# Expert V loads through an fp32 staging tile and a Pool cast, and the expert output added to the residual straight from PSUM

## The reference

```python
q = (h @ w_query).reshape(B, S, PEER_HEADS, 2, PEER_KEY_DIM)
...                                  # 16 of 16384 experts for each of 8 heads, idx and weight g
u = expert_u[it]
act = jax.nn.gelu(jnp.einsum('td,tkd->tk', xt, u))
return jnp.einsum('tk,tkd->td', gt * act, expert_v[it])
```

## Time and profile before

| | |
|---|---|
| time, median of 3 runs | 5994.31 us (5993.89 to 6028.91) |
| profiled execution, its own time | 5995.51 us |
| span of its slowest core (core 5) | 5994.0 us |
| spans of the eight cores | 5978.2 to 5994.0 us |
| first and last matmul of the expert stage | 4107.3 and 5947.7 us |
| PE, DVE, ACT, POOL busy over the span | 57%, 60%, 35%, 3% |

### The profile page before, as it was taken

The page is one execution under the profiler, slowest core; times in us unless marked ns, Lnnn a source line. Parts: engine busy times, 40 slices in busy tenths (PEclk is TensorE's granted clock), DMA queues, the critical chain, the costliest instruction groups (busy, mean ns, idle before and its releaser), DMA issues.

```text
span 5994.0 us, 76025 instructions; the slowest of 8 cores (5978.2 to 5994.0 us)
## 1 busy us (share of the span) xinstructions
PE 3400.3 (57%) x21200; PEld 2093.6 (35%) x21200; DVE 3620.7 (60%) x7629; ACT 2119.5 (35%) x4835; POOL 208.8 (3%) x399
## 2 busy tenths in 40 slices
PE   3333442566644631111121545446999999999996
PEld 1111111344422321111111222224666666666664
DVE  5777653555532338888878999995444444444445
ACT  3555431344421310100011767662333333333333
POOL 0000001000000000000000000001010010000000
PEclk7666665666656765555555555557999999999998
DMA  3112003000021010000000111124343343344332
GB/s 75 42 43 91 0 0 69 18 11 15 8 46 18 1 32 1 0 1 0 0 1 1 85 85 85 85 99 96 71 87 70 64 85 75 64 81 79 68 64 82
DMA packets 101513, 284.26 MB, mean 47 GB/s; under 512 B 9328, under 2 KB 11632, under 8 KB 98928
## 3 DMA queue, kind: packets, MB, share of 16 engines
q0 software_dynamic: 48144, 87.58, 9.7%
q1 hardware_dynamic: 52960, 191.82, 9.2%
HBM read 291.42 MB, written 75.50 MB: 61 GB/s over the span
## 4 chain that ended last, share of the span: by engine, by line
PE 45%; DVE 26%; issue 14%; ACT 10%; DMA 5%; DVEq 0%; ACTq 0%; POOL 0%; POOLq 0%; SPq 0%
PE ps_pO L1101 15%; PE ps_pA L253 15%; PE ps_pj L253 6%; ACT sb_rig L1018 3%; DVE sb_ohj L1010 3%; PE ps_pjb L253 3%; DVE sb_eqi L1013 2%; DVE sb_n_junk L211 2%; DVE sb_eq L973 1%; DVE sb_eq L969 1%; ACT sb_PT L643 1%; PE ps_pW L1029 1%; PE ps_pO L647 1%; DVE sb_sc L934 1%; PE ps_pPT L640 1%
## 5 line engine op out<-in xcount | busy, mean ns | idle before, releaser
L1101 PE MATMUL ps_pO<-sb_vt,sb_gw 128*128 128x512 bf16 x4096 | 1091.8, 379 | 19.0
L1090 DVE TENSOR_TENSOR sb_gw<-sb_ge,sb_wsl 128x256 bf16<-128x256 f32 x1024 | 434.6, 424 | 1057.9 <-PE ps_pO L1101 999.8
L253 PE MATMUL ps_pA<-sb_hfT,sb_ut 128*128 128x256 bf16 x8192 | 1063.5, 273 | 2.2 <-DVE sb_hfT L228 2.2
L253 PEld LDWEIGHTS ps_pA<-sb_hfT,sb_ut 128*128 128x128 bf16 x8192 | 801.7, 98 | 299.7 <-issue 2.4
L1088 ACT ACTIVATE sb_ge<-ps_pA 128x256 f32<-128x256 f32 x1024 | 399.5, 390 | 1207.2 <-PE ps_pA L253 1010.4
L1029 PE MATMUL ps_pW<-sb_rig,sb_ohj 128*128 128x128 bf16 x2048 | 380.9, 288 | 392.7 <-DVE sb_rig L1022 218.2
L1101 PEld LDWEIGHTS ps_pO<-sb_vt,sb_gw 128*128 128x128 bf16 x4096 | 400.1, 98 | 349.4 <-issue 100.4
L1029 PEld LDWEIGHTS ps_pW<-sb_rig,sb_ohj 128*128 128x128 bf16 x2048 | 205.4, 123 | 568.3 <-issue 567.4
L986 PE MATMUL ps_pTs<-sb_ident_f,sb_isel 128*128 128x128 f32 x16 | 7.1, 447 | 693.1 <-DVE sb_isel L976 693.1
L1115 DVE TENSOR_TENSOR sb_x_res<-sb_stage,sb_x_res 128x512 f32<-128x512 f32 x512 | 342.7, 690 | 29.1 <-ACT sb_stage L1109 3.3
L1034 ACT ACTIVATE sb_Wst<-ps_pW 128x512 bf16<-128x512 f32 x512 | 282.0, 593 | 219.7 <-PE ps_pW L1029 210.1
(11 more groups left out here) (208 smaller groups left out, 5090.9 us busy)
## 6 DMA issues: line engine op xcount, KB each, us to landing
wd_scratch<-sb_Wst SPq DMA_DIRECT2D x16, 4096.0 KB, 11.6
sb_wsl<-wd_scratch SPq DMA_DIRECT2D x128, 512.0 KB, 4.4
sb_ut<-uT POOLq DMA_DIRECT2D x128, 256.0 KB, 4.7
sb_vt<-ev POOLq DMA_DIRECT2D x128, 256.0 KB, 4.6
sb_xtmp<-xprev SPq DMA_DIRECT2D x48, 512.0 KB, 3.8
sb_x_res<-xown SPq DMA_DIRECT2D x16, 512.0 KB, 16.4
sb_xtmpb<-xown SPq DMA_DIRECT2D x16, 512.0 KB, 3.5
y<-sb_ot SPq DMA_DIRECT2D x16, 512.0 KB, 2.7
```

The source lines that it names most:

```text
L253: k.op("pe", lambda e, l=l, rh=rh, i=i: e.matmul(out_ap, lhsT=l, rhs=rh, start=(i == 0), stop=(i == n - 1)), r=r, w=w)
L1090: k.op("dve", lambda e: e.tensor_tensor(out=gw_[:].rearrange("p (a t) -> p a t", a=2), in0=ge_[:].rearrange("p (a t) -> p a t", a=2), in1= ...
L1101: k.op("pe", lambda e, po=po, t=t, half=half: e.matmul(po[:], lhsT=gw_[:, t * 128:(t + 1) * 128], rhs=v_[:, i, half * 512:(half + 1) * 512 ...
```

## The change

Three things change, all in the expert stage. `vt` gets one resource per slice (`nres=GS`), and line 1101's matmul of slice i waits only for that slice. V is loaded by `load_v`: SP issues a DMA of one slice in fp32 into one of three staging tiles `vstg`, used in turn, and POOL copies it to `vt`, which makes it bf16. The staging tile is free again when POOL's copy is done. At the end of a block ACT's copies and the tile `stage` are gone: DVE adds each `pO` tile to `x_res`.

```diff
--- before.py
+++ after.py
@@ -1049,12 +1049,21 @@
                 NG = 128 // GS
                 hfT = sb(pc, "hfT", [128, 8, NT], BF16)
                 ut = [sb(pc, "ut%d" % i, [128, GS, 8, 128], BF16) for i in range(2)]
-                vt = [sb(pc, "vt%d" % i, [128, GS, D], BF16) for i in range(2)]
+                vt = [sb(pc, "vt%d" % i, [128, GS, D], BF16, nres=GS) for i in range(2)]
+                vstg = [sb(pc, "vstg%d" % i, [128, D], F32) for i in range(3)]
+                vsc = [0]
+
+                def load_v(v_, i_, gi):
+                    st_ = vstg[vsc[0] % 3]
+                    vsc[0] += 1
+                    k.dma("sp", st_[:], ev_v[:, gi, :], r=[], w=[st_.res], sres=st_.res)
+                    k.op("pool", lambda e: e.tensor_copy(out=v_[:, i_, :], in_=st_[:]), r=[st_.res], w=[v_.rs[i_]])
+
                 uT_v = uT_d.rearrange("(i p) (c e) -> p i c e", p=128, c=8)
                 ev_v = ev_d.rearrange("(i e) d -> e i d", e=128)
                 for i_ in range(GS):
                     k.dma("pool", ut[0][:, i_, :, :], uT_v[:, i_, :, :], r=[], w=[ut[0].res], sres=ut[0].res)
-                    k.dma("pool", vt[0][:, i_, :], ev_v[:, i_, :], r=[], w=[vt[0].res], sres=vt[0].res, max_dma_last_dim=4096)
+                    load_v(vt[0], i_, i_)
                 with ExitStack() as pcn:
                     pTn = [ps(pcn, "pT4%d" % i, [128, 8, 128], BF16) for i in range(2)]
                     norm_pairs([(x_res[:, tile, :], x_res.rs[tile], pTn[tile % 2], hfT[:, :, tile * 128:(tile + 1) * 128], hfT.res)
@@ -1065,7 +1074,6 @@
                 wsl = [sb(pc, "wsl%d" % i, [128, 2, GS, 128], BF16) for i in range(2)]
                 ge = [sb(pc, "ge%d" % i, [128, T3], F32) for i in range(3)]
                 gw = [sb(pc, "gw%d" % i, [128, T3], BF16) for i in range(3)]
-                stage = [sb(pc, "stage%d" % i, [128, 2, D], F32, nres=4) for i in range(2)]
                 wd_v = wd_d.rearrange("t j (i x) -> j t i x", i=128)
                 items = [(g, tb, i) for g in range(NG) for tb in range(NT // T3) for i in range(GS)]
                 state = {}
@@ -1076,7 +1084,7 @@
                     if tb == 0 and i == 0 and g > 0:
                         for i_ in range(GS):
                             k.dma("pool", u_[:, i_, :, :], uT_v[:, g * GS + i_, :, :], r=[], w=[u_.res], sres=u_.res)
-                            k.dma("pool", v_[:, i_, :], ev_v[:, g * GS + i_, :], r=[], w=[v_.res], sres=v_.res, max_dma_last_dim=4096)
+                            load_v(v_, i_, g * GS + i_)
                     if i == 0:
                         ws_ = wsl[(g * (NT // T3) + tb) % 2]
                         k.dma("sp", ws_[:], wd_v[:, 2 * tb:2 * tb + 2, g * GS:(g + 1) * GS, :], r=[], w=[ws_.res], sres=ws_.res)
@@ -1100,22 +1108,15 @@
                             po = pO[t * 2 + half]
                             k.op("pe", lambda e, po=po, t=t, half=half: e.matmul(
                                 po[:], lhsT=gw_[:, t * 128:(t + 1) * 128], rhs=v_[:, i, half * 512:(half + 1) * 512],
-                                start=(i == 0), stop=(i == GS - 1)), r=[gw_.res, v_.res], w=[po.res])
+                                start=(i == 0), stop=(i == GS - 1)), r=[gw_.res, v_.rs[i]], w=[po.res])
                     if i == GS - 1:
-                        stg = stage[(g * (NT // T3) + tb) % 2]
-                        for t in range(2):
-                            for half in range(2):
-                                po = pO[t * 2 + half]
-                                k.op("act", lambda e, po=po, t=t, half=half: e.activation(
-                                    out=stg[:, t, half * 512:(half + 1) * 512], in_=po[:], func=AF.Copy),
-                                    r=[po.res], w=[stg.rs[t * 2 + half]])
                         for t in range(2):
                             tile = tb * 2 + t
                             for half in range(2):
-                                k.op("dve", lambda e, t=t, tile=tile, half=half: e.tensor_tensor(
-                                    out=x_res[:, tile, half * 512:(half + 1) * 512], in0=stg[:, t, half * 512:(half + 1) * 512],
-                                    in1=x_res[:, tile, half * 512:(half + 1) * 512],
-                                    op=ALU.add), r=[stg.rs[t * 2 + half], x_res.rs[tile]], w=[x_res.rs[tile]])
+                                po = pO[t * 2 + half]
+                                k.op("dve", lambda e, po=po, tile=tile, half=half: e.tensor_tensor(
+                                    out=x_res[:, tile, half * 512:(half + 1) * 512], in0=po[:], in1=x_res[:, tile, half * 512:(half + 1) * 512],
+                                    op=ALU.add), r=[po.res, x_res.rs[tile]], w=[x_res.rs[tile]])
 
                 emitA(0)
                 emitA(1)
@@ -1123,7 +1124,7 @@
                     if n + 2 < len(items):
                         emitA(n + 2)
                     emitV(n)
-                k.barrier(release=[t_.res for t_ in ut + vt + wsl])
+                k.barrier(release=[t_.res for t_ in ut + wsl + vstg])
 
         with ExitStack() as p4:
             gfin = sb(p4, "gfin", [128, D], F32)
```

## The result

The changed kernel takes 6426.84 us (median of 10 runs, 6422.51 to 6498.59) against 5997.12 (10 runs): the ratio is 1.0711, 95% interval 1.069 to 1.0732. It is slower, by 430 us where 373 were forecast, and inside the range. The profiled execution has a span of 6422.7 us against 5994.0, 428.7 more.

The account below looks back on a forecast made before the run. PE was taken to bound the expert stage, waiting only for emptied pO tiles at block starts and weights at group starts. 5995.5 + 192 (pO release) + 181 (V path) = 6368 us, range 6250 to 6510.

Parts of the forecast that it names:

- The `pO` release: Block ends: DVE's adds free the tiles, so PE's fourth V matmul starts 1.51 us later; 127 block starts, +192 us.
- behind the multiply: Block ends, DVE's order: the four adds stand behind the multiply of item 9, as before, so their schedule stays.
- The V path: Group starts: U loads end late behind POOL's first cast; 15 gaps of 9.1 us plus low clock, +181 us.
- T: Time at which part A of group g+1 would start if its weights were there.
- the clock: Behind each group-start gap PE runs slow, 2.9 us lost until the clock is back; 15 times, 44 us.
- The rival of the shared port: POOL's casts and DVE's two-SBUF-input multiplies exclude each other, holding multiplies up to 1.3 us; 6383 us; chance 0.15.
- The rival of the clock: PE's clock falls at block ends too, 2.9 us a time in a third of 127; 6736 us; chance 0.05.
- Hidden loads: Group starts: U at 3.5 us a slice or faster ends by T, leaving only the pO term; 6188 us; chance 0.08.
- Much later loads: POOL does cast and U-load descriptors one after the other, 6.1 us a slice; 6504 us; chance 0.15.
- Faster: Block ends: DVE frees tiles sooner than ACT, the 0.47 us stall goes, loads still fit; 5935 us; chance 0.02.

Follow-up runs that it names:

- The run with the adds first: Kernel before with DVE's adds from PSUM alone, plus the multiply of item n+2 emitted after the four adds at a block's end: 6082 and 6084 us.
- the run without casts: Kernel before with only the adds taken from PSUM, V still loaded by POOL's DMAs: 6187 us.
- the run with U first and ACT's copies: Changed kernel with ACT's copies of pO restored and all eight U loads ahead of the first cast: whole time not measured; four cores took 5998 to 6008 us.
- the split run: Kernel before, with ACT copying pO tiles 0, 1 and 3 and DVE adding tile 2 from PSUM first: 5936.9 and 5937.4 us.

## Why the prediction was right, and where its sizes were off

**What bounds.** PE's chain, as said, with the two places at which it can be made to wait. These two waits are 190.5 + 172.2 = 363 of the 428.7 us; most of the rest is low clock and a late instruction of ACT, below.

**The `pO` release, +192 forecast.** 127 x (15.86 - 14.36) = 190.5 us, and 190 for that part alone. The step-by-step times held: adds 0.72 apart in the mean, 0.14 us from an add's end to the matmul against 0.15. The run with the adds first shows the step "behind the multiply" by itself.

**The V path, +181 forecast.** The mechanism was right, three sizes were off. In the mean of the 15 groups, on the slowest core, V slice 0 was issued 31.4 us ahead of T, 30.9 forecast. It landed after 6.5 us, 5.0 forecast: that term was mis-sized by 1.5 (on half of the cores it was 5.1 to 5.2, as forecast). The cast took 1.06, 1.3 forecast. The seven U loads took 34.8 us to the last landing, 33.6 forecast. PE's first matmul follows the last landing by 0.25 us, which the sum left out. So the wait was 172.2 / 15 = 11.5 us, 9.1 forecast: 35 us more in all. Behind it the first block of a group is 17.8 us in the mean in place of 15.86: 28 us for the clock, 44 forecast; the 2.9 us that I took from the start of the stage was too much. That the sum came within 57 us of the measured difference owes a little to this: one size too small and one too large.

**A slip in the bounds.** With U at 5.6 us a slice the prediction's own figure is T + 14.7, so the upper bound of the V path is 15 x 14.7 + 44 = 265 and not 240, and that of the sum 6471 and not 6447. The range of 6250 to 6510 holds either.

**The rival of the shared port (0.15).** It happened, beside the forecast. In the changed kernel's timeline a multiply that meets a cast takes 1.39 us (DVE and POOL rows at the first cast of group 2):

```profile
4359.36 1.39 DVE L1098 TENSOR_TENSOR sb_gw<-sb_ge,sb_wsl 128x256 bf16<-128x256 f32 x1 [1.31 <-PE ps_pO L1109]
4359.42 1.05 POOL L1060 CAST sb_vt<-sb_vstg 128x1024 bf16<-128x1024 f32 x1
4361.17 0.43 DVE L1098 TENSOR_TENSOR sb_gw<-sb_ge,sb_wsl 128x256 bf16<-128x256 f32 x1 [0.41 <-PE ps_pO L1109]
```

Of 1024 multiplies 45 take over 0.6 us, 31 us above their usual 0.425 together; in the kernel before and in the run without casts none does. The adds, with one SBUF input, stay at 687 ns. The Trainium skill, SBUF — State Buffer, section Who interferes with whom, states that a DVE instruction with two SBUF inputs contends with a GpSimd instruction that reads SBUF. The trace agrees: the multiply beside the cast is 0.96 us longer than the one behind it, and the cast takes 1.05. Ahead of the stage two of DVE's instructions on `x_res` are held too: one of 1.22 us takes 2.42, one of 0.75 takes 1.68. From the first U load to the first A it is 58.6 us where it was 54.7: 4 us, up to 10 forecast. With both causes undone (the run with U first and ACT's copies) all of it together costs 12 to 17 us, 15 forecast.

**The rival of the clock (0.05).** It happened in a small part. At a dozen block ends the clock falls and the block takes 17.8 us. Rows at one of them: the GELU of the item whose multiply stands ahead of the adds, then PE's third and fourth V matmul and the A behind, then the busy time of the stretch that follows (columns as in the earlier trace rows); ahead of them the same GELU at a block end of 15.86 us:

```profile
4160.52 0.38 ACT L1096 ACTIVATE sb_ge<-ps_pA 128x256 f32<-128x256 f32 x1 [1.35 <-PE ps_pA L253]
...
4572.10 0.38 ACT L1096 ACTIVATE sb_ge<-ps_pA 128x256 f32<-128x256 f32 x1 [1.63 <-PE ps_pO L1109]
...
4575.29 0.38 PE L1109 MATMUL ps_pO<-sb_vt,sb_gw 128*128 128x512 bf16 x1 [0.22 <-DVE sb_x_res L1117]
...
4576.08 0.59 PE L1109 MATMUL ps_pO<-sb_vt,sb_gw 128*128 128x512 bf16 x1 [0.42 <-DVE sb_x_res L1117]
...
4576.46 0.85 PE L253 MATMUL ps_pA<-sb_hfT,sb_ut 128*128 128x256 bf16 x3
...
4576.00:4579.00 3.00, 2.92 (x11) 1.72 (x12) 0.27 (x1) 0.39 (x1) 0.00 (x0) 0.51 0.00 0
```

Three matmuls of 256 columns take 0.85 us, 0.49 elsewhere, and the granted clock is 0.51, 1.2 GHz. Away from the group starts the blocks over 15.86 us hold 30 of the 428.7 us, which with 190.5 + 172.2 + 28 + 4 makes 425.

The traces show what sets them off, and it is mostly not the casts. Every 32nd GELU starts 0.28 us late on ACT, as at 4572.10 (1.63 us of idle time in place of 1.35). In the changed kernel it is the second item of the third and of the seventh block of each group, just the one whose multiply DVE runs ahead of the adds. Those blocks take 16.14 us where nothing else happens, in the first group's third block too, where no cast runs; and 11 of the 12 falls of the clock are at these block ends, only two of them in blocks with casts. On all eight cores 76 of 77 falls are there. In the run with the adds from PSUM alone the late GELU is one item further on, off PE's path, and the eight cores have 5 falls together; with two staging tiles and with one resource per U slice no such GELU is late, and there are 20 and 12. What delays it no view shows, so this part of the time is an accident of where it falls in ACT's order, and the rival's mechanism (a longer wait at a block end lets the clock fall) is seen almost only where 0.28 us are added to the 1.5.

**The other rivals.** Hidden loads: no, though a resource per U slice made them so. Much later loads, with cast and descriptors in turn: no, U loads are 5.2 us apart where that rival had 6.1. Faster: the gain that I bounded at 60 us exists (the split run has it), but takes both engines: there the last tile is free 1.57 us after ACT's first copy starts, where ACT alone takes 2.06 and the four adds end 3.6 us after it.

## What to carry to other kernels

An instruction that takes over the freeing of a buffer is to be timed from its place in its engine's order, not by its length: four adds, each hardly longer than a copy (0.69 us against 0.61), but 0.72 us apart and on an engine with a multiply ahead of them, cost 1.5 us a block. A prefetch that is split over two queues starts when the later one lets it: look at what stands ahead on each queue, and at loads that wait for each other only because they share a resource. When two engines can each empty part of PSUM in time and neither can do all, share it. A time left over by a sum of waits is to be looked for block by block: here a third of a microsecond on ACT, twice in eight blocks, was most of it.

## What was not expected of the hardware

U loads that land after 8.4 us each instead of 4.5, with up to three more of them in flight, still have the last one of group 1 issued 22.5 instead of 32.4 us after the first cast: in the chain a slice takes 5.2 us, without it 3.0, in the mean of the groups.

Two staging tiles are as good as three (6421 and 6415 against 6427 us).

One GELU in 32 starts 0.28 us late, at a fixed place of the program, in the changed kernel and in the run with the adds from PSUM alone. On PE's chain it costs those 0.28 us, and in 11 of the 32 places on the slowest core a further 1.7 us of low clock; beside the chain it costs nothing.
